# A hybrid attention and gated-linear-attention layer: the second batch's norm woven into the first batch's last FFN products, attention's steps reordered at the tile's edge, and two PSUM banks for state updates

## What is computed

```python
hc = modulate(rms_norm(ctx, norm1_g[l]), sh1c, sc1c)
hx = modulate(rms_norm(x, norm1_g[l]), sh1, sc1)
aq, ak, av, gq, gk, gv, gg, glr, mg = split_in(hx @ w_in[l])
attn_x = latent_attention(q_x, concat([k_c, k_x]), concat([v_c, v_x]))
gla_x, _, _ = gla_bidir(*gla_heads(gq, gk, gv), la_f, la_b, s_f, s_b)
x = x + g1 * branch_merge(attn_x, gla_x, gg, mg, gla_norm_g[l], w_attn_proj[l], w_gla_proj[l], w_out[l])
x = x + g2 * swiglu(modulate(rms_norm(x, norm2_g[l]), sh2, sc2), w_ffn_in[l], w_ffn_out[l])
```

## Time and profile before

| what | value |
|---|---|
| time of the runs | median 3372.35 us of three (3370.74, 3372.35, 3610.68) |
| the profiled execution | 3392.19 us |
| its span on the slowest core (core 4) | 3391.1 us |
| spans of the eight cores | 3363.3 to 3391.1 us |
| mean granted clock of PE | 0.955 (core 4) to 0.965 of 2.4 GHz |
| PE busy / weight loads | 2976.9 us (88%) / 1593.1 us (47%) |
| ACT / DVE / POOL busy | 1371.7 us (40%) / 1260.2 us (37%) / 392.1 us (12%) |
| the chain that ended last, by engine | PE 77%, DVE 7%, ACT 7%, issue 5%, DMA 2% |
| HBM traffic | 290.77 MB read, 37.75 MB written, 97 GB/s over the span |

### The profile page before, as it was taken

How to read it: one execution, slowest core, us unless ns; L and a number is a source line. 1 busy time by engine, 2 the same in 40 slices (tenths; PEclk the granted TensorE clock), 3 DMA queues, 4 the chain that set the end, 5 groups by cost and what they waited for, 6 DMA issues and landing times.

```text
span 3391.1 us, 54218 instructions; the slowest of 8 cores (3363.3 to 3391.1 us)
## 1 busy us (share of the span) xinstructions
PE 2976.9 (88%) x18764; PEld 1593.1 (47%) x19088; DVE 1260.2 (37%) x2290; ACT 1371.7 (40%) x2420; POOL 392.1 (12%) x708
## 2 busy tenths in 40 slices
PE   6668787888899989999994888788889999899999
PEld 1145554555544444444443555455554444444444
DVE  0145664444232252122223566544433225322212
ACT  0155567777821132101105555677784112310110
POOL 0022231000000001101100123200000000110110
PEclk9789999999999987899996999999999999899999
DMA  8450120010132257634425012001002224773442
GB/s 251 134 159 14 26 57 20 8 26 7 25 51 38 38 162 130 94 93 91 72 87 139 14 26 51 20 14 26 7 14 51 38 38 124 159 115 94 90 72 87
DMA packets 97795, 234.26 MB, mean 69 GB/s; under 512 B 9524, under 2 KB 14007, under 8 KB 97271
## 3 DMA queue, kind: packets, MB, share of 16 engines
q0 software_dynamic: 62560, 131.36, 21.4%
q1 hardware_dynamic: 34968, 99.41, 9.7%
HBM read 290.77 MB, written 37.75 MB: 97 GB/s over the span
## 4 chain that ended last, share of the span: by engine, by line
PE 77%; DVE 7%; ACT 7%; issue 5%; DMA 2%; POOL 1%; DVEq 0%; SPq 0%; ACTq 0%; POOLq 0%
PE ps L1408 9%; PE ps L1415 9%; PE ps L1437 9%; PE ps L1319 6%; PE ps L1326 6%; PE ps L1193 6%; PE ps L1177 5%; PE ps L710 3%; PE ps L1298 3%; ACT sb_arenaB L1184 3%; PE ps L739 3%; PE ps L978 3%; PE ps L1365 3%; PE ps L463 2%; DVE sb_arenaB L1202 1%
## 5 line engine op out<-in xcount | busy, mean ns | idle before, releaser
L1184 ACT ACTIVATE sb_arenaB<-ps 128x1024 bf16<-128x1024 f32 x576 | 570.3, 1023 | 99.7 <-PE ps L1177 87.1
L1193 PEld LDWEIGHTS ps<-sb_arenaB 128*128 128x128 bf16 x4608 | 304.3, 97 | 196.4 <-issue 76.2
L1193 PE MATMUL ps<-sb_arenaB 128*128 128x129 bf16 x4608 | 355.2, 219 | 46.1 <-DVE sb_arenaB L1202 45.3
L1419 ACT ACTIVATE sb_arenaB<-ps 128x512 f32<-128x512 f32 x176 | 105.1, 597 | 666.6 <-PE ps L1408 666.5
L1408 PE MATMUL ps<-sb_hxT,sb_wbuf 128*128 128x512 bf16 x1376 | 342.3, 390 | 2.2 <-issue 0.4
L1415 PE MATMUL ps<-sb_hxT,sb_wbuf 128*128 128x512 bf16 x1382 | 340.5, 388 | 1.5
L1420 DVE TENSOR_TENSOR sb_arenaA<-ps,sb_arenaB 128x512 bf16<-128x512 f32 x176 | 121.8, 692 | 520.7 <-PE ps L1415 509.0
L1437 PE MATMUL ps<-sb_arenaB,sb_arenaA 128*128 128x512 bf16 x1380 | 303.1, 379 | 1.5
L1177 PE MATMUL ps<-sb_arenaB 128*128 128x512 bf16 x898 | 275.6, 378 | 21.0 <-ACT sb_arenaB L1184 13.9
L1319 PE MATMUL ps<-sb_hxT,sb_wbuf 128*128 128x512 bf16 x1004 | 240.2, 379 | 1.1
L1326 PE MATMUL ps<-sb_arenaA,sb_wbuf 128*128 128x512 bf16 x1002 | 239.8, 379 | 1.2
(11 more groups left out here) (189 smaller groups left out, 3810.9 us busy)
## 6 DMA issues: line engine op xcount, KB each, us to landing
sb_wbuf<-wfi POOLq DMA_DIRECT2D x176, 256.0 KB, 4.5
out<-sb_arenaA POOLq DMA_DIRECT2D x64, 512.0 KB, 4.6
sb_arenaA<-w_ada SPq DMA_DIRECT2D x12, 2048.0 KB, 18.4
sb_arenaA<-x SPq DMA_DIRECT2D x48, 512.0 KB, 8.1
sb_wbuf<-wb POOLq DMA_DIRECT2D x72, 256.0 KB, 4.2
sb_arenaA<-out SPq DMA_DIRECT2D x32, 512.0 KB, 3.7
sb_arenaB<-wfo POOLq DMA_DIRECT2D x22, 512.0 KB, 7.9
sb_arenaB<-x SPq DMA_DIRECT2D x16, 512.0 KB, 4.6
```

The lines of the kernel that those rows point to most:

```text
L1184: S.op("act", lambda e: e.activation(out=PT, in_=pS, func=AF.Exp, scale=ATT_SCALE, bias=-ATT_SHIFT), reads=pS_ks, writes=[PT_k])
L1193: last = e.matmul(oAll[:, sub, 0:129], lhsT=PT[:, x, sub * 128:(sub + 1) * 128], rhs=Vt[:, j, g, 0:129], start=(j == 0 and sub % 2 == 0), ...
```

## The change

Three edits.

**The norm of batch 1 moves.** `norm1` makes the four norm functions for a given batch. Before the last eight token tiles of batch 0's FFN (H = 1), the code now fetches head 0's weights (`prefetch(0)`), makes rings for the norm in places that are free there (four x tiles in arena B, eight normalised tiles in three arenas, PSUM banks 0 to 3), and weaves the whole norm of batch 1, with its transposes, as side items between the 16 units of FFN output products. The batch loop then makes its norm itself only for b = 0; for b = 1 head 0's items hold `lowrank` and no transposes. The decay weights `wlr` are loaded once.

**Attention.** In the last step of a tile, `pv` is now emitted before `qk`, so that `finish_o` follows an earlier `pv`. The output's transposes go from step 3 to step 2. Of the query work, the pieces of a tile begin at step 0 (with a piece of two products) instead of step 1, the stats' finish, norm and transposes one step later than before (the transposes at step 5 instead of 4).

**Banks.** In heads 0 to 3 `upd` has banks 6 and 7, and the ring of all other products has banks 2 to 5 (four instead of five).

```diff
-        rr = {"r": Ring(banks[2:7])}
+        rr = {"r": Ring(banks[2:6])}
...
-        rr["u"] = Ring(banks[7:8])
+        rr["u"] = Ring(banks[6:8])
...
+            if h == 0 and c < 3 and b > 0:
+                z_ = [(lambda: lowrank(c + 1), 1.8)] + z_
+                pre_ = []
+            elif h == 0 and c < 3:
...
-        prefetch(0)
-        S.dma("pool", wlr_sb, wlr_d, owner=wlr_k, writes=[wlr_k])
-        nstate = {}
-        cx = nc_n(0)
-        nstate[0] = nx_n(0)
-        nc_t(0, cx)
+        if b == 0:
+            prefetch(0)
+            S.dma("pool", wlr_sb, wlr_d, owner=wlr_k, writes=[wlr_k])
+            nstate = {}
+            cx = nc_n(0)
+            nstate[0] = nx_n(0)
+            nc_t(0, cx)
...
-                late = [u0 + 4, u0 + 5, u0 + 6, u0 + 7, u0 + 8]
+                late = [u0 + 4, u0 + 5, u0 + 6, u0 + 7, u0 + 9]
             else:
-                u0 = 9 * (n - 1) + 1
+                u0 = 9 * (n - 1)
                 if n == 4:
-                    u0 += 2
+                    u0 += 3
                 else:
-                    ends = [2, 4, 5, 6, 7, 8]
-                late = [u0 + len(ends), 9 * n, 9 * n + 1, 9 * n + 2, 9 * n + 4]
+                    ends = [2, 3, 4, 5, 6, 7, 8]
+                late = [9 * n - 2, 9 * n, 9 * n + 2, 9 * n + 3, 9 * n + 5]
...
+                if s == NP - 1:
+                    pv(g, s, PT, PT_k)
                 if s + 2 < NP:
                     qk(g, r, qTs[gi][0], qTs[gi][1], s + 2, ti)
...
-                pv(g, s, PT, PT_k)
-                if s == 3 and o_tr is not None:
+                if s < NP - 1:
+                    pv(g, s, PT, PT_k)
+                if s == 2 and o_tr is not None:
...
+            nside = []
+            if H == 1 and b + 1 < nb:
+                prefetch(0)
+                st_n, _ = AB.ring(11264, 3, [128, 12], F32, "nst")
+                xr_n, _ = AB.ring(12288, 4, [128, D], F32, "nxr")
+                xn_a, _ = AX.ring(0, 4, [128, D], BF16, "nxa")
+                xn_b, _ = AW.ring(1024, 2, [128, D], BF16, "nxb")
+                xn_c, _ = AA.ring(15360, 2, [128, D], BF16, "nxc")
+                mc_n, mc_t, mx_n, mx_t = norm1(b + 1, xr_n, Ring(xn_a.items + xn_b.items + xn_c.items), st_n, Ring(banks[0:4]))
+                ns = {}
+                nside = [(lambda: ns.update({-1: mc_n(0)}), 1.0), (lambda: ns.update({0: mx_n(0)}), 1.0)]
+                nside += [(lambda kt=kt: mc_t(0, ns[-1], [kt]), 0.5) for kt in range(KT)]
+                for g in range(4):
+                    if g < 3:
+                        nside.append((lambda g=g: ns.update({g + 1: mx_n(g + 1)}), 1.0))
+                    nside += [(lambda g=g, kt=kt: mx_t(g, ns[g], [kt]), 1.0) for kt in range(KT)]
+            fmain = []
             for tl in range(8):
...
+            weave(fmain, nside, 0.95)
```

More of the change, by code:

```diff
@@ L633, in build @@
         rz_r, off = AB.ring(off, 4, [128, 4], F32, "rz")
-        wgv = []
-        for i_ in range(2):
-            ap, tk, _ = AW.new(1024 * i_, [128, KT, 256], BF16, "wgv%d_" % i_)
-            wgv.append((ap, tk))
         wlr_sb, wlr_k = wlr_buf
@@ L1444, in build, with fload, fout, mmf @@
-                S.dma("pool", out_d[b, i * 128:(i + 1) * 128, :], stg, owner=stg_k, reads=[stg_k], writes=[x1d_k[i]], final=True)
+                bx = {}
+                def fload(i=i, bx=bx):
+                    xr6, xr6_k = xr6_r.next()
+                    S.dma("sp", xr6, out_d[b, i * 128:(i + 1) * 128, :], owner=xr6_k, reads=[x1d_k[i]], writes=[xr6_k])
+                    bx["x"] = (xr6, xr6_k)
+                    bx["s"] = stg_r.next()
+                fmain.append((fload, 0.0))
+                for cc in range(2):
+                    def fout(tl=tl, cc=cc, bx=bx):
+                        pF, pF_k = bF.next()
+                        xr6, xr6_k = bx["x"]
+                        stg, stg_k = bx["s"]
+                        def mmf(e):
+                            last = None
+                            for j in range(NJ):
+                                last = e.matmul(pF, lhsT=uT[:, j, tl * 128:(tl + 1) * 128], rhs=WoG[:, j, cc * 512:(cc + 1) * 512], start=(j == 0), stop=(j == NJ - 1))
+                            return last
+                        S.op("pe", mmf, reads=[uT_k[tl // 4]] + WoG_kj, writes=[pF_k])
+                        S.op("dve", lambda e: e.tensor_tensor(out=stg[:, cc * 512:(cc + 1) * 512], in0=pF, in1=G12[:, b, 1, cc * 512:(cc + 1) * 512], op=ALU.mult),
+                             reads=[pF_k, G12_k], wpart=[stg_k])
+                        S.op("dve", lambda e: e.tensor_tensor(out=stg[:, cc * 512:(cc + 1) * 512], in0=stg[:, cc * 512:(cc + 1) * 512], in1=xr6[:, cc * 512:(cc + 1) * 512], op=ALU.add),
+                             reads=[xr6_k, stg_k], wpart=[stg_k])
+                    fmain.append((fout, 1.0))
```

57 lines of the change are left out of this document (25 added, 32 removed).

## The result

The kernel before takes 3375.76 us (median of five, 3370.74 to 3811.5), the changed kernel 3227.32 us (median of five, 3225.16 to 3233.99). The ratio is 0.9572, with a 95% interval of 0.9554 to 0.959: 4.3% faster, some 145 us (3372.35 to 3227.32). The prediction was 3238 us in a range of 3200 to 3290. In some executions one half of the chip ran slower; ratios leave those out, for both kernels, and without them the kernel before is at 3372.35 us.

What follows compares the result with a forecast made beforehand. Idle PE time in batch 1's norm and head 0, the heads and attention was taken to bound the kernel. The terms -43 - 78 - 14 = -135 us, off the 3372 us median, gave 3238 us, range 3200 to 3290.

Steps and rivals of the forecast that it cites:

- the row-by-row construction of the rest: Batch 1's norm and head 0: 55 us built from profile rows would stay of 122.3, so 67 us gone.
- Part 1: Batch 1's norm woven into batch 0's last FFN output products: -67 + 9.5 + 15 = -43 us.
- The two waits and the unit behind them: Start of the woven stage: PE waits 3 and 7 us; with 1 for the second group, 4 for lower clock, 15.
- Part 2: Attention's new order: 1.49 us a tile at 23 edges in a batch, -78 us over two batches.
- `pv` first: Attention's tile edge, `pv` of step 8 ahead of `qk`: the next tile's `pv` starts 0.28 us earlier.
- The transposes' 0.84 us: Attention, output and query transposes three steps apart: L1161's 0.68 us wait goes, 0.84 by when PE could issue.
- the 0.43 of the query piece: Attention's tile edge: PE does two products of the query piece before the next `pv`, 0.43 us a tile.
- Part 3: Banks in the heads: 28 us gained at the update bank, 14 us more ring waits, net -14 us.
- ACT did not take attention over: Rival in attention: exps of 9.7 us a tile make ACT the limit, half the gain lost, 3277 us; chance 0.13.
- The norm was not short of data: Rival in the woven norm: slow loads and four-tile ring give 45 us of waits, not 15, 3268 us; chance 0.10.
- PE did not fall to its lower level: Rival in the woven stage: all units at 1.2 instead of 2.4 GHz, 76 us more, 3314 us; chance 0.04.
- The ring of four: Rival in the heads: some 294 bank takings, a third 0.6 us late each, 176 us, 3400 us; chance 0.03.

Runs made afterwards that it cites:

- the ring of four alone: Kernel before with banks 2 to 5 for the other products, updates still in bank 7 alone, bank 6 unused in the heads: ratio 1.0068.
- the kernel with both mends: Changed kernel with key transposes one item earlier and first x loads, squares and scalings in the FFN input products (context pair 8, latent group pair 19): ratio 0.9578.

## Why the prediction held, and where it was off

**What bounds the kernel.** Right. The three places with idle PE were the three that gave, and nothing outside them did. The gap in batch 1's norm was worth what the row-by-row construction of the rest said.

**Part 1, predicted -43, in stages -42 to -45, alone -45 (of which some is the clock in batch 1's heads).** Three terms were off and nearly cancel. The 144 transposes cost 8.0 us, not 9.5: inside a dense stage pairs start 0.11 us apart. The two waits and the unit behind them cost 11.8 us, not 15: my two places and sizes were right, but the loads came in 6.0 us, not 11, so that no later group waited. Head 0 took 59.4 us, not 55; the cores that had it at full clock took 57.0 us, and 55.7 in the norm-only run, which puts more than half of that on the granted clock (0.94), and not on a step left out.

**Part 2, predicted -78, measured -85.** The term that was mis-sized is `pv` first: 0.28 us for a tile, where it is 0.43, since the multiplications on DVE do not hold the reciprocal back. The 0.06 us left to ACT did not come either. The transposes' 0.84 us stands (0.83), and the 0.43 of the query piece fits the remainder of 0.44. By stretches the pieces are 23, 23 and 40 us.

**Part 3, predicted -14, measured -17.6 in stretches and -11.5 by itself.** The sum was right by luck, since both terms were too small by about as much: the second update bank brings 34 us (predicted 28), and the fifth bank of the ring costs 23 (predicted 14). The prediction had L844 and L710 grow. They did not; the new wait is at `amat`, a third user of the ring, with ACT's copy of the key transposes as releaser. To find that before a run I would have had to count banks back from each product through the woven order, and not scale the waits that are there. Nor had I a term for the clock, which is nearly half of the ring's price in the stretches.

**The rivals.** ACT did not take attention over: at `qk` and `pv` it holds PE for 9.1 + 13.4 = 22.5 us, against 20.8 in the norm-only run, whose attention is that of before. The norm was not short of data. PE did not fall to its lower level for the woven stage: its mean granted clock is 0.96 and one unit is slow, which is what these waits cost, 1.2 us. The ring of four costs 23 us and not 176; spread over the 294 products I had counted, that is 0.08 us for each, below the 0.5 from which it would decide.

**What stays open.** What sets the granted clock of the heads, which differs between kernels and between cores of one execution where PE's idle time is the same. The query piece by itself was not run. Why the scan product's wait for POOL grows from 15.9 to 22.5 us with two update banks was not tried either; with banks alone it is 23.3, with the ring of four alone 16.3, so it belongs to the second update bank. A likely reason, not tested, is that PE comes to the scan product sooner, and POOL's state is then what is late.

## What to carry to other kernels

Work that is woven into a dense stage costs its products, and beside them the waits of the engines that also free the stage's banks: an operation whose data is still in flight must not stand in the queue ahead of one that frees a bank. Issue the first loads a stage earlier, and look at which transfers they then meet. When a bank moves from one ring to another, price both ends separately and count back through the order who gets whose bank; the new wait can come at a product that had none. Look at every core before a difference of a few microseconds is put down to an edit: the slowest core may only be one whose clock was lower.

## What the runs showed of the hardware

The clock behind a short wait is not the same each time. After the same two waits of 1.67 us one core of the changed kernel ran eight products at 2.87 us and another at 1.91. This is `lowrank` in batch 1's head 0 with the `zdec` and `bdec` that wait ahead of it, on core 1 and then on core 2:

```profile
1734.06 2.87 PE L661 MATMUL ps<-sb_hxT,sb_wlr 128*64 128x512 bf16 x8
```

```profile
1723.83 1.91 PE L661 MATMUL ps<-sb_hxT,sb_wlr 128*64 128x512 bf16 x8
```

Over the whole of that head 0 PE is idle for 8.4 to 9.1 us on every core, and busy for 47.9 to 48.6 us at clock 1.00 on three cores and for 51.3 to 52.4 at 0.92 to 0.94 on the other five. A price for the clock behind such a wait is therefore an average.

Two cores of one die can be granted 0.81 of the clock for a while, with PE fully busy. In the kernel before, cores 4 and 5 had it from 1297 to 1410 us; this is the table of stretches on core 5, then on core 6:

```profile
1297.00:1410.00 113.00, 113.00 (x431) 46.75 (x430) 18.61 (x27) 17.41 (x28) 21.08 (x36) 0.81 0.69 117
```

```profile
1297.00:1410.00 113.00, 113.00 (x525) 51.21 (x524) 22.63 (x33) 20.98 (x34) 24.25 (x42) 1.00 0.84 131
```

431 recorded products against 525 in the same 113 us: a ratio of 0.82, the clock's own. Within the stretch the value is 0.81 in every window of a few microseconds, so it is no mix of long stretches at the two levels 1.2 and 2.4 GHz. Nor is it a mix of short ones: on core 5 each product starts 0.26 us after the one before, on core 6 0.21 or 0.22. The two other cores of that die, 6 and 7, had 1.00 all the while. It came again in the kernel with both mends, on cores 6 and 7 from 2049 to 2200 us, and costs the core some 18 to 20 us each time. The other cores ran the same instructions at 1.00 or 0.98, so the kernel alone did not call for it; whoever takes a baseline from a core that had it gives the change 20 us too much.
